# Attention scores in two products over stacked halves of k, with q staged by DMA

## The reference

```python
# l0: 8 heads, 2 kv heads, all 768 keys (context queries: the 256 context keys)
s = jnp.einsum('bqkgd,btkd->bkgqt', qblk, k, preferred_element_type=jnp.float32) * scale
p = jax.nn.softmax(s, axis=-1).astype(v.dtype)
return jnp.einsum('bkgqt,btkd->bqkgd', p, v)
# l1: 16 heads, 4 kv heads; band |q-k| <= 128 by blocks of 128 keys, all context keys, a sink logit
s_w = jnp.where(m[None, None, None], s_w, -jnp.inf)
p = jax.nn.softmax(jnp.concatenate([s_w, s_c, s_s], axis=-1), axis=-1).astype(v.dtype)
```

## Time and profile before

| | us |
|---|---|
| median of 3 runs | 2983.06 (2981.47 to 2984.42) |
| the profiled execution | 2983.85 |
| its span, first to last instruction | 2982.1 |
| PE busy in it | 2851.0 (96%) |
| DVE, ACT, POOL busy | 1622.1, 1026.2, 1240.2 |
| attention l0, first score to the start of the next projection | 198.6 to about 317 |
| attention l1 | 1119.1 to 1289.3 |
| attention s | 2193.9 to 2251.8 |

### The profile page before, as it was taken

The page is one execution under the profiler, slowest core; times in us unless marked ns, Lnnn a source line. Parts: engine busy times, 40 slices in busy tenths (PEclk is TensorE's granted clock), DMA queues, the critical chain, the costliest instruction groups (busy, mean ns, idle before and its releaser), DMA issues.

```text
span 2982.1 us, 41854 instructions
## 1 busy us (share of the span) xinstructions
PE 2851.0 (96%) x15434; PEld 2389.0 (80%) x15434; DVE 1622.1 (54%) x2521; ACT 1026.2 (34%) x1862; POOL 1240.2 (42%) x926
## 2 busy tenths in 40 slices
PE   8969999999999979999999999999999989999998
PEld 6859878888888769987888878888788757788886
DVE  6578887454555766665556553444543774422223
ACT  3248331121211426743222332222453673222222
POOL 1347323232323256644445444445364325344443
PEclk7979999999999999999999999999999989999999
DMA  5100424323232020042444424433202213123221
GB/s 210 57 26 33 143 77 149 106 98 113 98 113 92 22 79 2 2 143 98 173 150 153 157 85 148 154 141 133 95 20 92 85 50 113 57 85 106 96 94 57
DMA packets 78456, 290.95 MB, mean 98 GB/s; under 512 B 8833, under 2 KB 8961, under 8 KB 76929
## 3 DMA queue, kind: packets, MB, share of 16 engines
q1 hardware_dynamic: 78338, 289.36, 27.3%
HBM read 287.23 MB, written 2.10 MB: 97 GB/s over the span
## 4 chain that ended last, share of the span: by engine, by line
PE 84%; DVE 8%; issue 4%; POOL 2%; ACT 2%; DMA 0%; POOLq 0%; ACTq 0%; SPq 0%; DVEq 0%
PE ps L293 68%; PE ps L1222 4%; PE ps L1250 3%; PE ps L1238 2%; PE ps L493 2%; POOL w_lo L270 1%; PE ps L349 1%; DVE ps L600 1%; PE ps L1225 1%; DVE xl L607 1%; DVE rec L1645 1%; PE ps L954 1%; DVE r_g L1637 1%; DVE qn L1083 1%; PE ps L946 1%
## 5 line engine op out<-in xcount | busy, mean ns | idle before, releaser
L270 POOL TENSOR_TENSOR w_lo<-raw,w_hi 128x1024 fp32r<-128x1024 f32 x367 | 929.5, 2541 | 1454.7 <-ACT w_hi L264 1454.7
L264 ACT ACTIVATE w_hi<-raw 128x1024 fp32r<-128x1024 f32 x367 | 384.0, 1057 | 1356.5 <-PE ps L293 1247.2
L293 PE MATMUL ps<-n_hi,w_hi 128*128 128x512 f32 x1504 | 593.9, 395 | 12.2 <-DVE n_lo L1676 4.9
L293 PE MATMUL ps<-n_lo,w_hi 128*128 128x512 f32 x1504 | 586.8, 390 | 0.0
L293 PE MATMUL ps<-n_hi,w_lo 128*128 128x512 f32 x1504 | 586.6, 390 | 0.0
L819 DVE TENSOR_TENSOR y<-y,ps 128x512 f32<-128x512 f32 (+1 forms) x440 | 270.6, 632 | 266.3 <-PE ps L293 266.3
L338 DVE CUSTOM_DVE_ANT_0 dump<-modraw 128x1024 f32<-128x1024 f32 x212 | 357.2, 1685 | 15.4 <-DMA modraw<-mod_stream 9.9
L293 PEld LDWEIGHTS ps<-n_hi,w_hi 128*128 128x128 f32 x1504 | 283.4, 188 | 80.9 <-issue 11.7
L293 PEld LDWEIGHTS ps<-n_lo,w_hi 128*128 128x128 f32 x1504 | 283.4, 188 | 60.5 <-issue 2.7
L293 PEld LDWEIGHTS ps<-n_hi,w_lo 128*128 128x128 f32 x1504 | 283.3, 188 | 59.2
L774 DVE TENSOR_TENSOR ps<-ffn_silu,ps 128x512 f32<-128x512 f32 x110 | 68.5, 641 | 481.0 <-PE ps L293 464.8
(11 more groups left out here) (289 smaller groups left out, 4202.9 us busy)
## 6 DMA issues: line engine op xcount, KB each, us to landing
raw<-w_stream SPq DMA_DIRECT2D x367, 512.0 KB, 3.5
modraw<-mod_stream SPq DMA_DIRECT2D x152, 512.0 KB, 3.3
mod_pair<-mod_first SPq DMA_DIRECT2D x7, 1024.0 KB, 12.5
xl<-x_in SPq DMA_DIRECT2D x1, 2048.0 KB, 7.9
out<-xl SPq DMA_DIRECT2D x8, 256.0 KB, 2.1
xc<-ctx_in SPq DMA_DIRECT2D x1, 1024.0 KB, 10.0
modraw<-mod_first SPq DMA_DIRECT2D x1, 1024.0 KB, 15.1
rel<-rel_in SPq DMA_DIRECT2D x1, 1024.0 KB, 4.8
```

What stands on the lines that cost most here:

```text
L264: nc.scalar.activation(w_hi[:, c % RING, :], raw[:, c % RING, :], ACT.Copy).then_inc(hi_ready, 1)
L270: nc.gpsimd.tensor_tensor(w_lo[:, c % RING, :], raw[:, c % RING, :], w_hi[:, c % RING, :].bitcast(F32), ALU.subtract).then_inc(lo_ready, 1)
L293: mm = nc.tensor.matmul(out, w[a], x[b][:, off:off + n], start=first and i == 0, stop=last and i == 2)
```

## The change

Three things change, and what they need around them.

1. k is stored in halves: `k[0]` holds, for the head on rows 0 to 63, the high part on those rows and the low part on rows 64 to 127; `k[1]` the same for the other head, the other way round. ACT and DVE write each in two instructions of 64 rows. q is staged twice, the head's 64 rows of `q_hi` on both halves of `qs_hi`, those of `q_lo` on both of `qs_lo`. One matmul by `qs_hi` then gives hi by hi and hi by lo together, one by `qs_lo` the rest (lo by lo included).
2. Staging is no longer POOL's work but four DMAs of SP per unit, SBUF to SBUF, 64 rows of 512 bytes (`att_stage`). SP waits for the score product four units back. In l0 the modulation loads now stand between them in SP's order (`att_mod_loads`), and the last one behind the attention.
3. In l1 the context keys' scores are in the upper half of the first bank and the band, up to 384 keys, in the second, as one run.

The semaphores of the three attention stages become shared ones that count on.

```diff
     def in_act(act, st):
         def qk_hi(j, buf, n, ns):
...
-            nc.scalar.activation(buf[0][:, n, 0:w], qk_buf(st, j)[0][:, 0:w], ACT.Copy).then_inc(st["hi"], 1)
+            if buf is st["k"]:
+                for rows, u in zip(HALF_ROWS, buf):
+                    ins = nc.scalar.activation(u[rows, n, 0:w], qk_buf(st, j)[0][rows, 0:w], ACT.Copy)
+            else:
+                ins = nc.scalar.activation(buf[0][:, n, 0:w], qk_buf(st, j)[0][:, 0:w], ACT.Copy)
+            ins.then_inc(st["hi"], 1)
...
     def in_dve(dve, st, before_last=None):
-                nc.vector.tensor_tensor(buf[1][:, n, 0:w], q[:, 0:w], buf[0][:, n, 0:w].bitcast(F32), ALU.subtract
-                                        ).then_inc(st["lo"], 1)
+                if buf is st["k"]:
+                    for rows, other, u in zip(HALF_ROWS, HALF_ROWS[::-1], buf):
+                        ins = nc.vector.tensor_tensor(u[other, n, 0:w], q[rows, 0:w], u[rows, n, 0:w].bitcast(F32), ALU.subtract)
+                else:
+                    ins = nc.vector.tensor_tensor(buf[1][:, n, 0:w], q[:, 0:w], buf[0][:, n, 0:w].bitcast(F32), ALU.subtract)
+                ins.then_inc(st["lo"], 1)
...
+    HALF_ROWS = (slice(0, HD), slice(HD, P))
+    staged = [sem(f"staged{j}") for j in range(STAGED)]
...
         def qk(i):
-            pe.wait_ge(a["s_staged"], i + 1)
+            pe.wait_ge(staged[i % STAGED], 4 * 16 * ((a["u0"] + i) // STAGED + 1))
...
-                for j, (y, z) in enumerate(((0, 0), (0, 1), (1, 0))):
-                    mm = nc.tensor.matmul(score(i, col, w), (qs_hi, qs_lo)[y][:, i % STAGED, :], a["k"][z][:, kc, kcol:kcol + w],
-                                          start=j == 0, stop=j == 2 and not added)
+                for j, q in enumerate((qs_hi, qs_lo)):
+                    mm = nc.tensor.matmul(score(i, col, w), q[:, i % STAGED, :], k[:, kc, kcol:kcol + w],
+                                          start=j == 0, stop=j == 1 and not added)
...
+    def att_stage(sp, a, beside=None):
+
+        sp.wait_ge(lo_ready, a["next"] + RING)
+        for i, (c, x) in enumerate(a["units"]):
+            if i >= STAGED:
+                sp.wait_ge(a["s_qk"], a["u0"] + i - STAGED + 1)
+            else:
+                a["ready"](sp, c, x)
+            n = a["qchunk"](c, x)
+            for t, src in ((qs_hi, a["q"][0]), (qs_lo, a["q"][1])):
+                for rows in HALF_ROWS:
+                    sp.dma_start(t[rows, i % STAGED, :].bitcast(F32), src[HALF_ROWS[x[1]], n, x[2]:x[2] + P].bitcast(F32)
+                                 ).then_inc(staged[i % STAGED], 16)
+            if beside:
+                beside(i)
...
     def att_pool(pool, a):
-        def stage(i):
-            c, x = a["units"][i]
-            if i >= STAGED:
-                pool.wait_ge(a["s_qk"], i - STAGED + 1)
-            else:
-                a["ready"](pool, c, x)
-            n, half = a["qchunk"](c, x), x[1]
-            for t, src in ((qs_hi, a["q"][0]), (qs_lo, a["q"][1])):
-                ins = nc.gpsimd.tensor_tensor(t[:, i % STAGED, :], src[:, n, x[2]:x[2] + P].bitcast(F32),
-                                              blkones[:, half * HD:half * HD + 1].to_broadcast([P, P]), ALU.mult)
-            ins.then_inc(a["s_staged"], 1)
...
-                keys = [(0, S, C), (C, b0 * P, min(w, C))] + ([(2 * C, b0 * P + C, w - C)] if w > C else [])
+                keys = [(S - C, S, C), (S, b0 * P, w)]
...
     def s_in_act(act):
+            elif i < 8:
+                act.wait_ge(w_used, c0 + i + 1)
+                for rows, u in zip(HALF_ROWS, s_qkv[2:4]):
+                    ins = nc.scalar.activation(u[rows, i - 4, :], ps[rows, i % 4, :], ACT.Copy)
+                ins.then_inc(s_hi, 1)
...
     def s_in_dve(dve):
+            if 4 <= i < 8:
+                for rows, other, u in zip(HALF_ROWS, HALF_ROWS[::-1], s_qkv[2:4]):
+                    ins = nc.vector.tensor_tensor(u[other, i - 4, :], ps[rows, i % 4, :], u[rows, i - 4, :].bitcast(F32),
+                                                  ALU.subtract)
+                ins.then_inc(s_lo, 1)
+                continue
...
-        for c in range(MOD_FIRST, MOD_IN + MOD_RING):
+        for c in range(MOD_FIRST, MOD_FIRST + MOD_RING):
             load_mod(sp, c)
-        attention_stream(l0_att)
+
+        def att_mod_loads(i):
+
+            c = MOD_FIRST + MOD_RING + (i - 2) // (2 * ATT_MOD_EVERY) - 1
+            if i > 2 and (i - 2) % (2 * ATT_MOD_EVERY) == 0 and c < MOD_IN + MOD_RING:
+                load_mod(sp, c)
+
+        attention_stream(l0_att, att_mod_loads)
+        load_mod(sp, MOD_IN + MOD_RING - 1)
```

More of the change, by code:

```diff
@@ L1173, in pool_dve, with attention @@
             ins.then_inc(st["mix_lo"], 1)
-    def attention(name, units, q, k, v, out, qchunk, kchunk, vcol, outchunk, next_block, ready, extra=None, sink=None):
+    def attention(name, units, q, k, v, out, qchunk, kchunk, vcol, outchunk, next_block, ready, after=None, extra=None, sink=None):
         whole = [(c, x) for c in range(ATT_ITERS) for x in units]
@@ L1187, in attention @@
             groups.append([(0, (nb + 1) // 2), ((nb + 1) // 2, nb)] if nb > 1 else [(0, 1)])
-        cum = [0]
+        cum = [after["cum"][-1] if after else 0]
         for g in groups:
@@ L1192, in attention @@
                     outchunk=outchunk, ready=ready, extra=extra, sink=sink, groups=groups, cum=cum, n=len(whole), next=next_block,
-                    **{"s_" + s: sem(f"{name}_{s}") for s in (
-                        "qk", "negm", "p", "staged", "rinv", "norm", "t", "hi", "lo", "pv", "o", "m_hi", "m_lo")})
+                    u0=after["u0"] + after["n"] if after else 0,
+                    **{"s_" + s: sem(f"att_{s}") for s in (
+                        "qk", "negm", "p", "rinv", "norm", "t", "hi", "lo", "pv", "o", "m_hi", "m_lo")})
     ATT_ITERS = 4
+    HALF_ROWS = (slice(0, HD), slice(HD, P))
     STAGED = 4
+    staged = [sem(f"staged{j}") for j in range(STAGED)]
     def score(i, col, n):
@@ L1203, in score_width, with scores @@
         return P * len(a["units"][i][1][4]) + (1 if a["sink"] else 0)
+    def scores(a, i):
+        return score(i, a["units"][i][1][3][0][0], score_width(a, i))
     def turned(g, b0, b1):
@@ L1214, in qk @@
             c, x = a["units"][i]
-            keys = x[3]
+            keys, k = x[3], a["k"][x[1]]
             kc = a["kchunk"](c, x)
-            pe.wait_ge(a["s_staged"], i + 1)
+            pe.wait_ge(staged[i % STAGED], 4 * 16 * ((a["u0"] + i) // STAGED + 1))
             more = a["extra"](c, x) if a["extra"] else []
@@ L1227, in qk @@
                 n = a["sink"](c, x)
-                mm = nc.tensor.matmul(score(i, score_width(a, i) - 1, 1), ones[:, :], sinks[:, n:n + 1], start=True, stop=True)
+                mm = nc.tensor.matmul(score(i, keys[0][0] + score_width(a, i) - 1, 1), ones[:, :], sinks[:, n:n + 1], start=True, stop=True)
             mm.then_inc(a["s_qk"], 1)
         def turn(i):
-            pe.wait_ge(a["s_norm"], i + 1)
+            pe.wait_ge(a["s_norm"], a["u0"] + i + 1)
             for g, (b0, b1) in enumerate(a["groups"][i]):
@@ L1243, in values @@
             if i >= 2:
-                pe.wait_ge(a["s_o"], i - 1)
+                pe.wait_ge(a["s_o"], a["u0"] + i - 1)
             blocks = x[4]
@@ L1269, in exps @@
         def exps(i):
-            act.wait_ge(a["s_negm"], i + 1)
+            act.wait_ge(a["s_negm"], a["u0"] + i + 1)
             w, e = score_width(a, i), i % 4
-            nc.scalar.activation(prob[:, i % 2, 0:w], score(i, 0, w), ACT.Exp, bias=negm[:, e:e + 1],
+            nc.scalar.activation(prob[:, i % 2, 0:w], scores(a, i), ACT.Exp, bias=negm[:, e:e + 1],
                                  accum_out=rsum[:, e:e + 1]).then_inc(a["s_p"], 1)
@@ L1362, in att_pool @@
         pairs = a["n"] // 2
-        pool.wait_ge(lo_ready, a["next"] + RING)
-        for i in range(STAGED - 1):
-            stage(i)
         for i in range(a["n"]):
-            if i + STAGED - 1 < a["n"]:
-                stage(i + STAGED - 1)
             divide(i)
@@ L1375, in m_done @@
     def m_done(eng, a):
-        eng.wait_ge(a["s_m_lo"], a["n"] // 2)
+        eng.wait_ge(a["s_m_lo"], (a["u0"] + a["n"]) // 2)
     l0_att = attention(
@@ L1399, in l1_extra @@
         kc, t, b0, b1 = x[5]
-        return [(C + (b - b0) * P, P) + ((ident_r[:, :], mask[:, :]) if b < t else (mask[:, :], ident_r[:, :]))
+        return [(S + (b - b0) * P, P) + ((ident_r[:, :], mask[:, :]) if b < t else (mask[:, :], ident_r[:, :]))
                 for b in range(b0, b1) if b != t]
@@ L1761, in _, with attention_stream @@
         load_block(sp, 3)
-        def attention_stream(a):
-            sp.wait_ge(a["s_pv"], a["n"])
+        def attention_stream(a, beside=None):
+            att_stage(sp, a, beside)
+            sp.wait_ge(a["s_pv"], a["u0"] + a["n"])
         def stage(name):
```

31 lines of the change are left out of this document (16 added, 15 removed).

## The result

The kernel with the change is slower: 3043.41 us (median of 4 runs, 3036.91 to 3053.11) against 2982.26 us for the kernel before (median of 4 runs, 2978.68 to 2984.42). The ratio is 1.0209, its 95% interval 1.0179 to 1.0239. The profiled execution took 3053.11 us, its span is 3051.3, 69.2 over the span of before. I had forecast 2967.6 with a range of 2955 to 2984.

What follows compares the result with a forecast made beforehand. The prediction took PE (TensorE) to bound the kernel, being last in nearly every unit of l1 and s but not l0. Its terms, -6.2 -22.4 +5.3 +6.6 +1.2 = -15.5 us, gave 2967.6, range 2955 to 2984.

Steps and rivals of the forecast that it cites:

- Staging by DMA: Four SP copies per unit at 0.45 us an issue, 1.80 a unit; landing 2.1 us after issue, hidden.
- Rival 3: SP as the bound everywhere: an issue of 0.60 makes 2.4 us a unit, +29 us, 3012; decides from about 0.54; 12%.
- l1, -22.4: Score products in l1: PE's shorter work saves 22.4 us, the unit falling from 2.58 to 2.23.
- Rival 2: l1 gives half, PE waiting for the ACT and DVE loop: -4.3 us, 2978.8; 12% together with issues around 0.5.
- l0, -6.2: Score products in l0: 6.2 us saved, crediting only steps that wait for PE; bounds 2 to 13.
- Hidden: SP's issues in l0: 12x1.80 plus one or two modulation loads is 22.3 us, under 26.2, so no cost.
- s, +5.3: Attention stage s: SP becomes last at 1.80 us a unit against 1.63 before, costing 5.3 us over 32 units.
- Starts, +6.6: Start of each attention stage: first score 3.5 us after POOL's last weight split instead of 1.3, 6.6 us over three.
- k in halves, +1.2: Writing k chunks in two instructions delays the first q of l1 by 1.2 us, bounds 0 and +3; nothing in l0 and s.
- The clock, rival 4: PE gaps in s and the starts lower PE's clock; s wholly at the lower level gives +15 us, 2998; 6%.
- The sum: All terms over the three attention stages together: -15.5 us, span 2966.6, median 2967.6.

Runs made afterwards that it cites:

- lone: pool_half with one more copy in each of 48 units of l1, into a spare tile, held back to stand alone on SP; 2949.28 us, one run.
- merge2: The changed kernel with q's high and low parts side by side in one tile, so two staging copies a unit, not four; 2955.26 us, ratio 0.9948.
- pool_half: merge2 with the half that stays on its rows copied by POOL, so one SP copy a unit; 2947.91 us, ratio 0.9917; again 2948.48, 0.9901.
- band384: The kernel before with only l1's band of up to 384 keys as one run, three products kept; 2967.56 us, ratio 0.9977.
- probe: The changed kernel with l1's copies given other shapes for eight units each, most to a spare tile; 3030.15 us, one run.

## Why the prediction was wrong, point by point

**The step that failed** is the price of an issue in "Staging by DMA": "Nearest for the issue are SP's other issues ... I take 0.45". Measured 0.60, 0.64 from start to start. All the rows that I took were loads of 128 rows from HBM, and lone showed that this is the cheap form: 0.33 against 0.48 for 64 rows out of SBUF, before the 0.1 that a queue without pause adds to either. The text said that no row of before showed such a copy, and yet its bounds, 0.38 to 0.53, were those of the loads. A bound for a form that no row shows has to reach past the rows of another form. The rivals named the threshold, 0.54, and I gave the side beyond it 12%.

**Rival 3, the one that happened**, was priced at +29 us with 0.60 an issue. It came to +69: with 0.64 the unit is 2.56 and not 2.40 (0.16 x 141 units = 23 us), and the long issues add 19.8 (6.7 + 10.9 + 2.2), which the attention stages of before could not show, since SP issued almost nothing there. The two together are 42, and the difference was 40.

**l1, -22.4**: the reasoning was right and its place was taken. merge2 gives -21.3 and a unit of 2.23, PE without a gap. Rival 2, half the gain, is refuted by the same stretch.

**l0, -6.2**: right in size where SP is out of the way, -4.4 in merge2 and -5.2 in pool_half. "Hidden" was wrong in the changed kernel: 2.56 x 12 = 30.7 and a load or two against 26.2.

**s, +5.3**: here SP was forecast to be last, and was, by 2.64 us a unit and not 1.80. PE's own side was 5.1 forecast, 4.1 in pool_half and 2.7 in merge2.

**Starts, +6.6**: measured +8.4, 3.9 us from the split to the score where 3.5 was said. That part is the issues again, 3x0.64 in place of 3x0.45; the landing was 1.9 to 2.0. The rest lies in the kernel before: its first score follows the split by 1.31 in l1, but by 0.98 in l0 and s, where the prediction took 1.3 for all three.

**k in halves, +1.2**: the sign was right, the size less than half. From l0's last row maximum to the last split before l1 it is 807.64 us before and 807.10 after, and nothing is seen; but that stretch holds l0's FFN. Read where the cost was forecast, from the start of l1's last projection matmul to the end of the last split, it is 17.23 us in the kernel before and in band384, which write k whole, and 17.68 to 17.74 in all nine kernels that write it in halves: +0.5. It was not tried by itself.

**The clock, rival 4**: 0.91, 0.97 and 0.95 in the three stretches of the changed kernel, so it did fall, but behind a queue that was late anyway. By the Trainium skill ("TensorE: Matmul & The Clock Gate", What's actually happening) a PE that works less is throttled; the direction agrees with these windows, and it was an effect here and not the cause.

**The sum.** Put 0.64 and the long issues into my own steps and the outcome follows within about 1 us a stage. Apart from the first score of l0 and s the views were read rightly; one price was borrowed from another form of the same instruction.

## What to carry to other kernels

A transfer that is hidden as a landing still costs its issue on the queue that issues it: multiply the issues per step by the price of just that form, in a burst, and hold that against the step of the bounding engine. Where no row shows the form, let its bound reach well past its cheaper relatives, and if the sign of the change hangs on it, forecast the sign with that doubt. And when the copies are too many, put what lies side by side into one of them: halving their number turned +2.1% into -0.5%, and giving one of the two halves to an idle engine into -0.8 to -1.0%.

## What the runs showed of the hardware

- SP's issue of a copy costs 0.33 us (128 rows x 512 B or 4 KB from HBM, and 128 rows from SBUF to HBM), 0.52 (64 rows from HBM), 0.50 (128 rows from SBUF to SBUF), 0.48 (64), 0.57 to 0.59 (16 rows, or 64 rows with two pieces each); in a burst 0.43 for the first form and 0.59 to 0.61 for the copies of probe and merge2, whatever they hold. A modulation load right behind a staging copy costs 0.58 in the changed kernel, in pool_half, alone in the same stage, 0.33. POOL's queue takes 0.52 to 0.57 for such a copy. The Trainium skill ("DMA: Bandwidth & Descriptors", Anatomy of one DMA) gives about 50 ns for the dispatch of a DMA that GpSimd issues, and the prediction held that against SP's. No issue here was under 0.33 us on SP or under 0.52 on POOL.
- The long issues fall together with the fetches of instructions. The page counts 73 packets on the queue of kind instruction that moves 16 KB at a time (q8). On one clock, in the changed kernel, first fetches and issues of l1:

```
fetch starts      1153.5  1166.2  1178.0  1189.1  1204.6  1215.4  1227.0  1241.8
long issue from   1153.57 1166.40 1177.92 1189.39 1204.81 1215.64 1227.00 1241.76
its time          1.28    1.24    1.83    1.08    1.19    1.09    1.28    1.56
```

  The first eight are shown. 13 of 13 fetches in l1, 8 of 8 in l0 and 3 of 3 in s have a long issue that starts within 0.4 us of them, and there is no other long issue. In merge2, whose queue rests at times, it is 11 of 13 in l1. In pool_half, which issues a quarter of the time, no issue is longer than 0.80, although one was running during 10 of the 24 fetches: a fetch beside an issue is not enough, and long issues are seen only where copies follow one another. The fetches are 11 to 17 us apart in l1, four to six units. That the fetch is what lengthens the issue is an inference from this coincidence; no run moved the fetches.
- Whole times of this program carry two steps of about 5 and 10 us that belong to the start and to l0's FFN. Differences of a few us are better read from the starts of one instruction at both ends of a stage.
